# Gate logits in four column groups, and squares of the second norm summed on GpSimd

## The reference

```
h = RMSNorm(x) * (1 + scale1) + shift1
proj = h @ w_in                  # q, k, v of three mixers, gates, 32 small gate columns
A: gated DeltaNet    B: mLSTM    C: windowed attention
x += gate1 * (merge of A, B, C) @ w_out
h = RMSNorm(x) * (1 + scale2) + shift2
x += gate2 * ExpertChoiceSwiGLU(h)      # 16 experts
```

## Time and profile before

| | |
|---|---|
| median of 3 runs | 2004.76 us (2004.1 to 2005.08) |
| the profiled execution | 2002.95 us |
| span from its first to its last instruction | 2001.0 us |
| mean granted TensorE clock | 0.970 |
| TensorE busy, matmuls | 1840.5 us (92%) |
| VectorE busy | 731.4 us (37%) |
| ScalarE busy | 506.7 us (25%) |
| GpSimd busy | 110.8 us (6%) |
| HBM | 171 GB/s over the span |

### The profile page before, as it was taken

How to read it: one execution, slowest core, us unless ns; L and a number is a source line. 1 busy time by engine, 2 the same in 40 slices (tenths; PEclk the granted TensorE clock), 3 DMA queues, 4 the chain that set the end, 5 groups by cost and what they waited for, 6 DMA issues and landing times.

```text
span 2001.0 us, 27232 instructions
## 1 busy us (share of the span) xinstructions
PE 1840.5 (92%) x11453; PEld 1067.5 (53%) x11453; DVE 731.4 (37%) x1683; ACT 506.7 (25%) x997; POOL 110.8 (6%) x160
## 2 busy tenths in 40 slices
PE   5989999999899978999989899999999999799996
PEld 3658864455555553333355787545555555433333
DVE  2465411472441142322346543117615212423233
ACT  3444321321440120111145333213125202111112
POOL 2012100001000020000000120000100000000000
PEclk8999999999999979999989899999999998899998
DMA  9325403203204317999952352141131242299991
GB/s 329 134 85 181 171 4 119 53 22 134 87 2 167 126 49 277 428 426 427 407 186 86 127 181 86 53 113 30 51 129 43 84 168 84 74 413 428 427 427 69
DMA packets 96104, 344.47 MB, mean 172 GB/s; under 512 B 21114, under 2 KB 23378, under 8 KB 83568
## 3 DMA queue, kind: packets, MB, share of 16 engines
q1 hardware_dynamic: 93040, 338.36, 44.0%
q0 software_dynamic: 2944, 4.39, 1.0%
HBM read 339.31 MB, written 3.41 MB: 171 GB/s over the span
## 4 chain that ended last, share of the span: by engine, by line
PE 73%; DVE 9%; ACT 7%; DMA 6%; issue 2%; DVEq 2%; ACTq 0%; PEld 0%; SPq 0%; PEldq 0%
PE PS L670 15%; PE PS L1381 10%; PE PS L761 4%; PE PS L1404 4%; DMA ring<-in_w_expert_up_dram 4%; PE PS L1314 4%; PE PS L677 4%; PE PS L653 2%; PE PS L1101 2%; PE PS L1215 2%; PE PS L1299 2%; PE PS L1370 2%; PE PS L888 2%; PE PS L875 2%; PE PS L1358 2%
## 5 line engine op out<-in xcount | busy, mean ns | idle before, releaser
L670 PE MATMUL PS<-hT,ring 128*128 128x384 f32 x1216 | 406.8, 490 | 16.4 <-DVE arena L2244 6.4
L670 PEld LDWEIGHTS PS<-hT,ring 128*128 128x128 f32 x1216 | 228.7, 191 | 179.0 <-issue 14.7
L1432 ACT ACTIVATE arena<-PS 128x256 f32<-128x256 f32 (+5 forms) x398 | 168.5, 436 | 570.5 <-PE PS L653 205.9
L1381 PE MATMUL PS<-ring,arena 128*48 128x512 f32 x768 | 225.5, 593 | 1.2 <-DMA ring<-in_w_expert_up_dram 1.2
L761 PE MATMUL PS<-hT,ring 128*128 128x384 f32 x384 | 133.3, 504 | 8.8 <-DMA ring<-in_w_in_dram 7.0
L1381 PE MATMUL PS<-arena 128*48 128x512 f32 x256 | 112.6, 593 | 3.9 <-DVE arena L2332 2.2
L653 PE MATMUL PS<-const,arena 128*128 128x128 f32 (+2 forms) x553 | 89.0, 291 | 22.8 <-DMA arena<-in_x_sample_dram 8.6
L761 PEld LDWEIGHTS PS<-hT,ring 128*128 128x128 f32 x384 | 75.0, 198 | 60.5 <-issue 14.7
L1381 PEld LDWEIGHTS PS<-ring,arena 128*48 128x48 f32 x768 | 66.4, 123 | 76.5 <-issue 76.4
L2349 DVE TENSOR_TENSOR arena<-arena,PS 48x512 f32<-48x512 f32 x32 | 22.1, 690 | 227.2 <-ACT arena L1750 227.2
L1370 PE MATMUL PS<-arena 128*128 128x384 f32 x256 | 100.3, 511 | 4.7 <-ACT arena L1432 1.7
(11 more groups left out here) (313 smaller groups left out, 2337.6 us busy)
## 6 DMA issues: line engine op xcount, KB each, us to landing
ring<-in_w_expert_up_dram SPq DMA_DIRECT2D x32, 2048.0 KB, 18.6
ring<-in_w_in_dram SPq DMA_DIRECT2D x26, 2048.0 KB, 9.3
ring<-in_ada_w_dram SPq DMA_DIRECT2D x24, 2048.0 KB, 11.8
arena<-in_w_expert_gate_dram SPq DMA_DIRECT2D x16, 2048.0 KB, 13.8
ring<-in_w_expert_down_dram SPq DMA_DIRECT2D x16, 2048.0 KB, 16.2
ring<-in_w_expert_gate_dram SPq DMA_DIRECT2D x16, 2048.0 KB, 14.4
arena<-in_w_expert_down_dram SPq DMA_DIRECT2D x16, 2048.0 KB, 16.8
ring<-in_w_out_dram SPq DMA_DIRECT2D x4, 2048.0 KB, 10.5
```

The source lines that it names most:

```text
L670: ins = mm(out, w[:, k, 128 * c:128 * c + 128], hT[:, k, :], start=k == 0, stop=k == KT - 1)
L1381: ins = mm(PS[64 * n:64 * n + ROWS, u % 2, :], xsT[:, k, u, :], block_view(blk + n)[:, k, :], start=k == 0, stop=k == KT - 1)
L1432: return f(out, in_, ACT.Copy)
```

## The change

There are two independent parts.

*Gate logits.* After product 0 TensorE computes `gate_parts`: for each block k one product with the 32 columns of `w_small` as the stationary operand and all 384 tokens of `hT` as the moving one. Block k goes to column group k mod 4, so blocks k and k + 4 are summed in the same 32 partitions, and bank 7 holds four partial sums of 32 rows each. VectorE copies these to SBUF, into `rstd`, which is free there, between convolutions 0 and 1. After product 1 the new `gate_logits` takes three products with a 128x128 block of that copy as the stationary operand and a new constant `fold` (128x32, four identities on top of each other) as the moving one: this turns the logits to tokens by gates and adds the four parts.

*Squares.* GpSimd adds the squares of blocks 1 to 6 into that of block 0, each as soon as ScalarE has written it. TensorE's seven ones-products inside the out-projection loop go; behind the loop stand one ones-product with the sum and one with the square of block 7.

```
+    tabs["fold"] = (r % 32 == np.arange(32)[None, :])
...
-            "gate_pe": ["proj", "cum"], ... "gate_dve": ["biased", "lf", "args", "done"],
+            "gate_pe": ["part", "proj", "cum"], ... "gate_dve": ["part", "biased", "lf", "args", "done"],
-            "rt_pool": ["clear"],
+            "rt_pool": ["clear"], "sq_pool": ["sum"],
...
+                for k in range(1, KT - 1):
+                    pool.wait_ge(done["nrm_act"], at("nrm_act", l, ("sq1", k)))
+                    ins = nc.gpsimd.tensor_tensor(norm_sq[:, 0, :], norm_sq[:, 0, :], norm_sq[:, k, :], ALU.add)
+                    if k < KT - 2:
+                        pool.drain()
+                ins.then_inc(T["sq_pool"].mark("sum"), 1)
                 pool.wait_ge(done["nrm_pe"], at("nrm_pe", l, "ss1"))
...
+                def gate_parts():
+                    for n in range(2):
+                        for q in range(4):
+                            k = 4 * n + q
+                            ins = mm(PS[32 * q:32 * q + 32, 7, 0:N], w_small[:, k, :], hT[:, k, :], start=n == 0, stop=n == 1)
+                    ins.then_inc(T["gate_pe"].mark("part"), 1)
+
                 def gate_logits():
+                    pe.wait_ge(rest_in, 16)
+                    pe.wait_ge(done["gate_dve"], at("gate_dve", l, "part"))
                     for t in range(TILES):
-                        for k in range(KT):
-                            ins = mm(PS[:, 7, 32 * t:32 * t + 32], hT[:, k, 128 * t:128 * t + 128], w_small[:, k, :],
-                                     start=k == 0, stop=k == KT - 1)
+                        ins = mm(PS[:, 7, N + 32 * t:N + 32 * t + 32], rstd[:, 128 * t:128 * t + 128], K("fold"), start=True, stop=True)
                     ins.then_inc(T["gate_pe"].mark("proj"), 1)
...
                     blk = conv_channels(blk, j)
+                    if j == 0:
+                        gate_parts()
                     if j == 1:
                         gate_logits()
...
-                    if c:
-                        square_sum(l, 1, c - 1, 0)
-
-
-                square_sum(l, 1, KT - 1, 0)
+
+
+                pe.wait_ge(done["sq_pool"], at("sq_pool", l, "sum"))
+                mm(PS[:, 0, 0:N], ones, norm_sq[:, 0, :], start=True, stop=False)
+                pe.wait_ge(done["nrm_act"], at("nrm_act", l, ("sq1", KT - 1)))
+                mm(PS[:, 0, 0:N], ones, norm_sq[:, KT - 1, :], start=False, stop=True).then_inc(T["nrm_pe"].mark("ss1"), 1)
...
-                    TT(gates, PS[:, 7, 0:96].rearrange("p (t c) -> p t c", c=32), over(bias_b, 1, TILES), ALU.add)
+                    TT(gates, PS[:, 7, N:N + 96].rearrange("p (t c) -> p t c", c=32), over(bias_b, 1, TILES), ALU.add)
...
                 conv(0)
+                v.wait_ge(done["gate_pe"], at("gate_pe", l, "part"))
+                V.tensor_copy(rstd[:, :], PS[:, 7, 0:N]).then_inc(T["gate_dve"].mark("part"), 1)
                 conv(1)
```

More of the change, by code:

```diff
@@ L360, in build_step @@
             + [s for k in rng(KT) for s in [("xn1", k)] + [("h1", k)] * (k in BY_DVE[1])],
-            "gate_pe": ["proj", "cum"], "gate_act": ["exp", "ln", "ecum"], "gate_dve": ["biased", "lf", "args", "done"],
+            "gate_pe": ["part", "proj", "cum"], "gate_act": ["exp", "ln", "ecum"], "gate_dve": ["part", "biased", "lf", "args", "done"],
             "conv_pe": [s for j in rng(12) for s in [("p", j)] + [("ss", i) for i in LENGTHS.get(j, ())]],
```

## The result

| | before | after |
|---|---|---|
| median of 5 runs on one chip | 2004.76 us (2003.0 to 2008.56) | 1988.89 us (1988.72 to 1994.7) |
| the profiled execution | 2002.95 us | 1988.89 us |
| span | 2001.0 us | 1987.1 us |
| mean granted TensorE clock | 0.970 | 0.972 |
| TensorE busy | 1840.5 us | 1825.6 us |

The changed kernel is faster: the ratio is 0.9932, 95% interval 0.9913 to 0.9951. The same kernel run again (the last experiment) gave 1990.55 us, ratio 0.9926 (0.9912 to 0.994). The forecast was 1993.8 us with a range from 1990.5 to 1997.5. So the direction was right. By the ratio, which is not the quotient of these medians, the gain is 13.6 us and the time 1991.1 us, inside the range; its interval holds both.

A forecast was written before the change was run, and what follows sets the result against it. TensorE, holding 73% of the chain of waits, was taken as the bound. 2 x 3.9 + 0.8 + 3.2 = 11.8 us, less 0.8 for the clock, 11.0: 2004.76 - 11.0 = 1993.8 us, range 1990.5 to 1997.5.

The forecast's parts named there:

- Out-projection, 3.9 us a layer: Out-projection, both layers: six ones-products of 0.65 us leave TensorE, saving 3.9 us a layer.
- the cover: Out-projection end: the sum of blocks 0 to 6 is ready 2.4 us before product 7 ends.
- Gate products and turn, 1.45 and 0.66 us: Gate place: eight packed products take 1.45 us, by the modulation block's row; three logits products take 0.66 us instead of 5.28.
- The new wait, 2.4 and 1.6 us: Before the gate sums: TensorE, done earlier with product 2, waits 1.6 to 2.4 us for VectorE's `lf`.
- Product 3 starts 0.8 and 3.2 us earlier: Gate place: with the chain through `lf` counted, product 3 starts 0.8 us earlier in layer 0, 3.2 in layer 1.
- The step that failed: Gate place: product 3 was taken to run no longer than before, so its earlier start of 0.8 and 3.2 us counted fully.
- the clock falls in the new wait: Rival, before the gate sums: TensorE's standing lowers its clock, about 1.3 us per fall, 1996.4 us with both layers; chance 0.12.
- product 3 above 6 us in both: Gate place, both layers: product 3 taking over 6 us was listed as a sign that the prediction was wrong.
- 0.8 for the clock: Layer 1's gate place: deduction because only half of the 1.7 us clock fall was counted as regained; 11.8 became 11.0.
- GpSimd as the bound: Rival, out-projection: adds slower than 5.16 us make TensorE wait at the sum; 2012.8 us at 6.5 us an add; chance 0.02.
- groups that do not overlap: Rival, gate place: the column groups run one after another, parts take 5.2 us, gain 4.4, time 2000.4 us; chance 0.05.
- a swallowed gain: Rival, expert stage: transfers take back the out-projection's gain, only the gate's 3.2 us stays, 2001.6 us; chance 0.05.

## Why the prediction came out as it did

*Out-projection, 3.9 us a layer:* measured 3.74 in both layers and in every kernel with the squares. The adds took 0.99 us where 1.26 was taken from the smaller row, the cover was 2.8 us instead of 2.4, and no expert stage swallowed the gain.

*Gate products and turn, 1.45 and 0.66 us:* 1.43 and 0.59. The packed modulation block was the right row.

*The new wait, 2.4 and 1.6 us:* 1.88 and 1.57.

*Product 3 starts 0.8 and 3.2 us earlier:* from product 0 it started 2.29 and 2.96 us earlier. In layer 0 some 1.2 of that is product 0 itself, which took 6.83 us instead of some 8, so about 1.0 is the change's. The working holds in both layers. That it could start from a layer 0 without a fall in product 2 was chance: the other five profiled passes of that code all had one.

*The step that failed is the one that let product 3 run at 5.23 us.* The rival "the clock falls in the new wait", given 0.12, came true in both layers and cost 1.7 each, not 1.3; product 3 above 6 us in both was one of the prediction's own signs of being wrong. The argument for its low chance was that the out-projection ran at full rate after an idle of 1.35 us. The other half of that argument, the small products behind the wait, should have weighed more. The Trainium skill (TensorE: Matmul & The Clock Gate, Part 1) says that gaps bring the half rate back. The traces agree in 11 of the 14 passes with the wait, and the fall in layer 1 before, which the prediction took as agreeing, had no gap ahead of it. That fall is the second half of the mistake: the prediction counted it as regained by half, where it moved to product 3. So the gate places gave 0.60 and 1.27 us up to product 4, where 4.0 less 0.8 for the clock had been counted.

*What made up for it was not in the sum, and was luck.* 2.69 us came from the stop in layer 1's modulation, shown by padding to follow the position in the instruction stream; 3.59 us came from steps of the clock behind product 4 in layer 1, all of a size that the same code shows without the edit. With the forecast's own terms alone (7.5 from the squares, 1.9 from the gates) the gain would have been 9.4 us and the time near 1995.4, inside the range. The result lies at the lower end of the range (by the ratio) or below it (by the medians) through gains that the prediction had no case for.

*GpSimd as the bound, groups that do not overlap, a swallowed gain:* none happened. The second was tried and costs 7 to 11 us.

## What to carry to other kernels

Small work on a bound TensorE is worth moving to an idle engine when each piece is ready long before it is needed; leave the last piece where it was, since there the other engine's time and hand-over stand on the path (1.2 to 1.8 us here). When a change shortens TensorE's work between two steps of a slower chain, count the new wait and then look at the product behind it, and at the next stretch with pauses: a clock fall avoided in one place came back in another in three of four passes. Read the place that a forecast starts from in more than one pass, since layer 0 here was the exception among six. Before a gain of 1 to 3 us is credited to an edit, see whether the stage that holds it was touched at all.

## What the hardware showed unexpectedly

- TensorE stopped for 0.82 to 2.04 us in a modulation block, with no wait that the profile shows, at a place that moved with the number of instructions ahead of it: after 248 of 256 at position 105, 24 instructions later at position 81, and not visibly at 30 and 54; in layer 0 after 169, and after 206 with 181 places of padding.
- A clock fall in a product of 5.2 us mostly cost 1.7 us: 5.2 or 6.9, 5.40 or 7.09 us, also for the same instructions of the same kernel in two executions. Falls stood behind waits of TensorE, but not behind each (the same wait of 1.57 us was followed by 6.9 us five times and by 5.2 us twice), and in 5 of 6 passes behind 48 small instructions in 5.3 us without any wait.
- Eight fp32 products of 32 by 384 in four column groups took 1.43 us, in one group 5.28 us.
- A GpSimd addition of 128x384 fp32 took 0.99 us, against 0.84 for 128x256: half again as many elements cost 18% more.
